# A lead of 16 slots in place of 12 between dots and scaling, and the gelu of a batch at step 2 in place of step 4

## The chip, the core and the metric

The kernel runs on one core of one Trainium2 chip. The core has five engines with a program each: TensorE (PE: PE's matmuls and PEld's weight loads), VectorE (DVE), ScalarE (ACT), GpSimd (POOL) and SyncE (SP), and 16 DMA engines that move data between memory and the on-chip buffers. The engines wait for each other by semaphores. The metric is the device time of one execution in microseconds (us).

## What is computed

One encoder layer over 1024 tokens of width 1024, all in float32: a LayerNorm, a mixer (attention over latents with 8 heads, and a Fourier branch, merged by gates), a LayerNorm, and the channel part, in which each token takes 128 single-neuron experts out of 16,384:

```python
def peer(x, w_q, keys, w_u, w_v):
    xt = x.reshape(T, D)
    q = (xt @ w_q).reshape(T, PEER_HEADS, 2, PEER_HALF)
    s_half = jnp.einsum('thcd,hcnd->thcn', q, keys, ...)
    sv, si = lax.top_k(s_half, PEER_TOPK)
    cand = (sv[:, :, 0, :, None] + sv[:, :, 1, None, :]).reshape(...)
    cv, ci = lax.top_k(cand, PEER_TOPK)
    ...
    expert = (ia * PEER_NKEYS + ib).reshape(T, PEER_HEADS * PEER_TOPK)
    gate = jax.nn.softmax(cv, axis=-1).reshape(T, PEER_HEADS * PEER_TOPK)
    def run(blk):
        xc, ec, gc = blk
        u = jnp.take(w_u, ec, axis=0)
        h = jnp.einsum('cd,ced->ce', xc, u, ...)
        a = (jax.nn.gelu(h, approximate=False) * gc).astype(x.dtype)
        return jnp.einsum('ce,ced->cd', a, jnp.take(w_v, ec, axis=0))
```

For each token and each of its 128 experts a row of w_u (4 KB) and a row of w_v (4 KB) are read: 1024 x 128 x 2 x 4 KB, or 1.07 GB, of the 1.24 GB that the core moves in all.

## The kernel before

The 1024 tokens are four groups of two tiles of 128 tokens. A tile has 128 slots, one for each of a token's experts: slot i of a tile is the i-th expert of all of its 128 tokens, one on each partition. One gather (an indirect DMA that GpSimd starts) brings one row of w_u, or of w_v, to each partition, 512 KB. A group has 256 slots.

A slot passes five stations: GpSimd gathers its u row (L310); DVE multiplies it with the token and sums it up, the dot (L872); GpSimd gathers its v row (L319); ACT scales it by the slot's coefficient into one of two buffers av (L1099); PE adds it to acc by eight transposing matmuls (L600). Between dot and scaling, for eight slots at a time (a batch), ACT takes the gelu of the eight dots (L1090) and DVE multiplies it with the gates to the coefficients (L883). The scaling of a batch's first slot waits for them.

The order is written out by hand. Each engine runs through steps m = 0 to 255 of a group. At step m GpSimd gathers the u row of slot m + LEAD + AHEAD and then the v row of slot m + LEAD; DVE does the dot of slot m + LEAD + AHEAD; ACT scales, and PE adds, slot m + LEAD. LEAD is 64. A slot number past 255 is one of the next group, so the numbers run on from group to group. At step m of a batch's eight (m modulo 8) ACT takes the gelu at 4, DVE the coefficients at 5, both for the batch that starts at the next step 0. In one engine's program the steps follow in order; between engines there are only the semaphores.

There are six buffers for u rows and six for v rows. GpSimd waits at slot i for the dot of slot i - 6 (u_free) or for the scaling of slot i - 6 (scaled).

Beside this work of group g each engine does the "front" of group g + 1 in the same steps: attention in steps 0 to about 72 (scores, maximum on DVE at L760, exponential on ACT at L1030 every four steps, transposes, values), gates in 72 to 120 (sigmoid L1047), output projection to 136, LayerNorm, then queries of the experts to about 215. The group before all this (steps 0 to 255 of the first front) has no retrieval beside it till its own expert numbers are there. After the last group's start there is no front.

The expert numbers of a tile come from DVE in four pairs of heads, 32 slots each (`retrieve`): two top-16 searches for each head, and for each pair the numbers at L852, which gives the semaphore `handed`, the token's copy (L855) and the softmax of the gates, with an exponential on ACT at L1083. Tile 0 has its pairs at steps 171, 187, 203 and 219 of the front; tile 1 at steps 45, 69, 93 and 117 of the next round. The first gather of each 32 slots waits for `handed`. HAND0 and HAND1, worked out from AHEAD, are the steps at which the first gathers of tile 0 and tile 1 stand; ACT's load of the residual rows stands at step HAND1 + 2.

Of the kernel before, what the change touches and what calls it, by code (L numbers as in the profile page):

```python
# [35 lines left out]
SLOTS = PH * TOPK  # L36
STEPS = TILES * SLOTS
BATCH = 8
AHEAD = 12
LEAD = 64  # L40
PAIRS = PH // 2
PSLOTS = SLOTS // PAIRS
# [17 lines left out]
IDS = 3  # L60
HAND1 = SLOTS - AHEAD - LEAD
HAND0 = STEPS - AHEAD - LEAD
assert T0 + T_PERIOD + IDS + 3 < HAND0 and T_PERIOD <= PSLOTS // 2 and T0 + PH * T_PERIOD <= STEPS
# [4 lines left out]
def layer_program(nc, x, lnp, w_lat, w_z, w_kr, b_lat, b_zT, b_krT, gqkv, w_uk, w_uv, b_gate, wstream,  # L68
# [4 lines left out]
    with ctx:  # L73
# [168 lines left out]
        def has_slot(g, i, last):  # L242

            return i < STEPS and not (isinstance(g, int) and g < 0) or i >= STEPS and not last
# [45 lines left out]
        def _(pool):  # L290
# [13 lines left out]
            def gather_u(g, i):  # L304
                g, i = slot_of(g, i)
                if i % PSLOTS == 0:
                    pool.wait_ge(handed, g * TILES * PAIRS + i // PSLOTS + 1)
                pool.wait_ge(u_free, g * STEPS + i + 1)
                t, s = divmod(i, SLOTS)
                pool.indirect_dma_start(  # L310
                    u_rows[:, ring(g, i, NU), :], None, peer_u,
                    bass.IndirectOffsetOnAxis(ap=ids_peer[:, t, s:s + 1], axis=0)).then_inc(u_in[ring(g, i, NU)], 16)
# [10 lines left out]
            def peer(g, last):  # L323
                for m in range(STEPS):
                    if has_slot(g, m + LEAD + AHEAD, last):
                        gather_u(g, m + LEAD + AHEAD)
                    if has_slot(g, m + LEAD, last):
# [303 lines left out]
        def _(dve):  # L631
# [234 lines left out]
            def dot(g, i):  # L866
                g, i = slot_of(g, i)
                t = i // SLOTS
                dve.wait_ge(u_in[ring(g, i, NU)], landed(g, i, NU))
                row = u_rows[:, ring(g, i, NU), :]  # L870
                b = i // BATCH % 2
                v.tensor_tensor_reduce(out=row, in0=row, in1=h1_peer[:, t, :], scale=1.0, scalar=0.0, op0=ALU.mult,  # L872
                                       op1=ALU.add, accum_out=dots[:, b, i % BATCH:i % BATCH + 1]).then_inc(u_free, 1)
# [23 lines left out]
            def peer(g, m, last):  # L897
                if has_slot(g, m + LEAD + AHEAD, last):
                    dot(g, m + LEAD + AHEAD)
                if m % BATCH == 5 and has_slot(g, m + LEAD + BATCH, last):  # L900
                    coefs(g, (m + LEAD) // BATCH + 1)
# [42 lines left out]
        def _(act):  # L944
# [42 lines left out]
            for n in range(2 * FG):  # L987
                g, half = divmod(n, 2)
# [5 lines left out]
            for n in range(1, TT * FG, 2):  # L994
                tt, g = divmod(n, FG)
# [3 lines left out]
            for n in range(H):  # L999
                pair, half = divmod(n, 2)  # L1000
                act.wait_ge(k_ps, n + 1)
                for odd in range(2):
                    last = s.activation(KT[0:NOPE, 2 * pair + odd, half * 512:(half + 1) * 512],
                                        (m0, m1)[n % 2][odd * NOPE:(odd + 1) * NOPE, :], ACT.Copy)
# [81 lines left out]
            def gelu(g, k):  # L1086
                g, i = slot_of(g, k * BATCH)
                k = i // BATCH
                act.wait_ge(u_free, g * STEPS + NU + BATCH * (k + 1))
                s.activation(act_out[:, k % 2, :], dots[:, k % 2, :], ACT.Gelu).then_inc(act_done, 1)  # L1090
# [38 lines left out]
                        act.wait_ge(y_spilled[i], 16 * (FG // 2))  # L1129

            def gelus(g, m, last):
                if m % BATCH == 4 and has_slot(g, m + LEAD + BATCH, last):
                    gelu(g, (m + LEAD) // BATCH + 1)

            for m in range(STEPS):
                if has_slot(-1, m + LEAD, False):
                    scale(-1, m + LEAD)
                gelus(-1, m, False)
                front(0, m)
                dft(m)  # L1140

            def group(g, last):
                for m in range(STEPS):
                    for t in range(TILES):
                        if m + LEAD == (t + 1) * SLOTS:
                            evict(g, t)
                    if has_slot(g, m + LEAD, last):
                        scale(g, m + LEAD)
                    gelus(g, m, last)
                    gate_exp(g, 1, m, R0, R_PERIOD)  # L1150
                    if not last:
                        front(g + 1, m)
                    for t in range(TILES):
                        if m + LEAD == (t + 1) * SLOTS:
                            finish(g, t)
                        if m + LEAD == (t + 1) * SLOTS + 2:
                            store(g, t)
# [89 lines left out]
```

## Time and profile before

| | us |
|---|---|
| median of three runs | 3777.69 |
| lowest and highest | 3771.69 to 3777.8 |
| profiled execution, its own time | 3777.35 |
| its span in the trace | 3775.5 |
| busy: PE 2722.5, POOL 2360.9, DVE 2217.4, ACT 1600.3 | 72%, 63%, 59%, 42% of the span |
| q0, the gathers' DMA queue | 75.2% of 16 engines' span |
| first gather starts | 530.8 |
| mean granted TensorE clock | 0.808 of full speed |

The first 530 us are projections of all tokens and the first front; from there to the end the gathers run. A row of the profile names the line, the engine, the operation and `out<-in` by the program's names (`rows` holds the u and v buffers, `dots`, `coef`, `av` as above; `small` holds the row maximum among others). Behind a group, or in square brackets behind a row, stands the idle time of the engine before it, and what ended it. "issue" is a wait for nothing that the profile shows, "remote" one for something that it doesn't name. Times are from the start of the span.

### The profile page before, as it was taken

The numbers are of one execution on the slowest core, as the hardware profiler recorded it, in microseconds if no ns is written. First come the engines' busy times: TensorE is split into PE (matmuls) and PEld (weight loads), VectorE is DVE, ScalarE is ACT, GpSimd is POOL, SyncE is SP. The second block draws the span as 40 slices with busy tenths as digits, with TensorE's granted clock in tenths as the row PEclk, the third lists the DMA queues.
The fourth block names the chain that finished last, engine by engine and source line by source line (L and its number), as shares of the span: only waits on it lengthen the run. The fifth ranks groups of instructions, "written<-read, shape, count | busy, mean of one in ns | idle before, by whom it ended". The sixth has DMA issues, their size and how long they took to land.

```text
span 3775.5 us, 40818 instructions
## 1 busy us (share of the span) xinstructions
PE 2722.5 (72%) x14008; PEld 2179.7 (58%) x14008; DVE 2217.4 (59%) x5004; ACT 1600.3 (42%) x1836; POOL 2360.9 (63%) x2075
## 2 busy tenths in 40 slices
PE   6999966578788676577887775677986665565545
PEld 3456745456675565466775664566765554444444
DVE  5143067458765676477765685578655774467533
ACT  1121014345454444354554454454544453344434
POOL 4000028766677767766677787756776777677775
PEclk9999987578799886698898895787998885655656
DMA  4235459998999999998999999989999999999997
GB/s 167 86 106 173 151 171 353 356 348 314 345 409 409 392 363 356 362 342 330 358 409 404 375 379 350 359 319 331 399 409 391 381 343 351 349 357 345 353 359 291
DMA packets 350432, 1240.83 MB, mean 329 GB/s; under 512 B 38480, under 2 KB 46160, under 8 KB 349712
## 3 DMA queue, kind: packets, MB, share of 16 engines
q0 software_dynamic: 294912, 1073.87, 75.2%
q1 hardware_dynamic: 34096, 117.94, 8.5%
q10 hardware_dynamic: 21216, 46.40, 3.4%
q8 instruction: 111, 1.82, 0.2%
q14 instruction: 97, 0.79, 0.1%
HBM read 1222.33 MB, written 15.73 MB: 328 GB/s over the span
## 4 chain that ended last, share of the span: by engine, by line
PE 29%; POOL 24%; issue 13%; another core or an unknown queue 10%; DMA 8%; ACT 7%; DVE 6%; DVEq 3%; SPq 0%; ACTq 0%
POOL rows L319 12%; POOL rows L310 11%; PE acc L600 9%; DMA rows<-in_peer_v,ids_peer 7%; ACT av L1099 5%; PE fA L523 3%; PE m L567 2%; PE fA L483 2%; PE m L371 2%; PE m L499 2%; PE acc L589 1%; DVE rows L872 1%; PE fB L341 1%; PE fB L535 1%
## 5 line engine op out<-in xcount | busy, mean ns | idle before, releaser
L600 PE MATMUL acc<-ident,av 128*128 128x128 f32 x8192 | 1394.9, 331 | 904.3 <-ACT av L1099 587.2
L600 PEld LDWEIGHTS acc<-ident,av 128*128 128x128 f32 x8192 | 1176.8, 172 | 1137.8 <-ACT av L1099 692.5
L1099 ACT ACTIVATE av<-rows,coef 128x1024 f32<-128x1024 f32 x1024 | 1161.4, 1145 | 1479.6 <-DMA rows<-in_peer_v,ids_peer 563.5
L310 POOL DMA_INDIRECT rows<-in_peer_u,ids_peer x1024 | 1137.2, 1111 | 807.3 <-DVE ids_peer L852 339.5
L872 DVE CUSTOM_DVE_ANT_0 rows<-rows,hh 128x1024 f32<-128x1024 f32 x1024 | 1235.7, 1222 | 651.3 <-DMA rows<-in_peer_u,ids_peer 573.8
L319 POOL DMA_INDIRECT rows<-in_peer_v,ids_peer x1024 | 1175.6, 1148 | 444.0 <-issue 292.4
L567 PE MATMUL m<-hT_g,wring 128*128 128x256 f32 x1024 | 249.2, 400 | 1.1 <-ACT hT_g L1061 1.1
L523 PE MATMUL fA<-hT_g,wring 128*128 128x256 f32 x1024 | 241.7, 392 | 0.9 <-issue 0.9
L567 PEld LDWEIGHTS m<-hT_g,wring 128*128 128x128 f32 x1024 | 203.4, 204 | 29.7 <-ACT hT_g L1061 1.5
L523 PEld LDWEIGHTS fA<-hT_g,wring 128*128 128x128 f32 x1024 | 199.1, 199 | 29.0 <-issue 2.4
L768 DVE COPY S<-fB 128x1024 f32<-128x1024 f32 x64 | 78.2, 1222 | 151.9 <-PE fB L341 69.1
L499 PEld LDWEIGHTS m<-V,S 128*128 128x128 f32 x1024 | 145.1, 225 | 13.6 <-DVE S L768 7.8
L499 PE MATMUL m<-V,S 128*128 128x64 f32 x1024 | 146.2, 306 | 7.1 <-DVE S L768 6.6
L483 PE MATMUL fA<-KT,hT_g 96*128 96x512 f32 x256 | 131.5, 636 | 4.2 <-issue 4.0
L1030 ACT ACTIVATE S<-fA,small 128x1024 f32<-128x1024 f32 x64 | 71.0, 1110 | 117.0 <-DVE small L762 116.2
L535 PE MATMUL fB<-yo,wring 128*128 128x256 f32 x512 | 115.8, 379 | 0.0
L883 DVE TENSOR_TENSOR coef<-act_out,gate_peer 128x8 f32<-128x8 f32 x128 | 21.1, 165 | 140.1 <-ACT act_out L1090 86.0
L535 PEld LDWEIGHTS fB<-yo,wring 128*128 128x128 f32 x512 | 95.4, 190 | 12.0
L783 DVE TENSOR_TENSOR prod<-sg,fB 128x512 f32<-128x512 f32 x32 | 21.9, 683 | 135.9 <-PE fB L535 94.4
L760 DVE TENSOR_REDUCE small<-fA 128x1 f32<-128x1024 f32 x64 | 78.1, 1221 | 35.3 <-PE fA L483 17.4
L1090 ACT ACT_TABLE_LOAD x73 | 93.7, 1283 | 1.3
L341 PE MATMUL fB<-ident,S 128*128 128x128 f32 x512 | 83.4, 315 | 3.7 <-issue 3.6
(153 smaller groups left out, 2173.5 us busy)
## 6 DMA issues: line engine op xcount, KB each, us to landing
wring<-in_wstream SPq DMA_DIRECT2D x192, 512.0 KB
ln<-in_dft_seq ACTq DMA_DIRECT2D x32, 512.0 KB, 3.4
rows<-in_peer_u,ids_peer POOLq DMA_INDIRECT x1024
rows<-in_peer_v,ids_peer POOLq DMA_INDIRECT x1024
hT_g<-in_x SPq DMA_DIRECT2D x8, 512.0 KB, 3.6
hres_spill<-KT ACTq DMA_DIRECT2D x8, 512.0 KB, 2.7
hT_spill<-rows ACTq DMA_DIRECT2D x1, 4096.0 KB
wring<-in_wstream SPq DMA_DIRECT2D x16, 256.0 KB
```

Of the source, the lines that this page charges most:

```text
L310: pool.indirect_dma_start(u_rows[:, ring(g, i, NU), :], None, peer_u, bass.IndirectOffsetOnAxis(ap=ids_peer[:, t, s:s + 1], axis=0)).then_ ...
L319: pool.indirect_dma_start(v_rows[:, ring(g, i, NV), :], None, peer_v, bass.IndirectOffsetOnAxis(ap=ids_peer[:, t, s:s + 1], axis=0)).then_ ...
L341: return nc.tensor.transpose(out_, in_, ident[:, :])
L483: last = mm(fA[:, half * 512:(half + 1) * 512], qT_g[0:QK, h, tok(qt)], KT[0:QK, h, half * 512:(half + 1) * 512], start=True, stop=True)
L499: last = mm(m1[:, h * VD:(h + 1) * VD], probsT[:, tok(k)], V[:, k, h * VD:(h + 1) * VD], start=k == 0, stop=k == TT - 1)
L523: last = mm(gb[:, j * GROUP:(j + 1) * GROUP], w[:, tok(k)], hT_g[:, k, :], start=k == 0, stop=k == KD - 1)
L535: last = mm(yb[:, j * GROUP:(j + 1) * GROUP], w[:, tok(4 * j + k)], src[:, k, :], start=k == 0, stop=k == 3)
L567: last = mm(m0[:, (qc % 2) * GROUP:(qc % 2 + 1) * GROUP], w[:, tok(k)], hT_g[:, k, :], start=k == 0, stop=k == KD - 1)
L600: last = mm(acc[:, tok(k)], av[:, i % NAV, tok(k)], ident[:, :], is_transpose=True, start=i % SLOTS == 0 and k % 4 == 0, stop=i % SLOTS == ...
L872: v.tensor_tensor_reduce(out=row, in0=row, in1=h1_peer[:, t, :], scale=1.0, scalar=0.0, op0=ALU.mult, op1=ALU.add, accum_out=dots[:, b, i ...
L1090: s.activation(act_out[:, k % 2, :], dots[:, k % 2, :], ACT.Gelu).then_inc(act_done, 1)
L1099: s.activation(av[:, i % NAV, :], v_rows[:, ring(g, i, NV), :], ACT.Copy, scale=coef[:, b, i % BATCH:i % BATCH + 1]).then_inc(scaled, 1)
```

## The change

AHEAD goes from 12 to 16, and the gelu of a batch goes from step 4 of eight to step 2.

```diff
@@ -36,7 +36,7 @@
 BATCH = 8
-AHEAD = 12
+AHEAD = 16
 LEAD = 64
@@ -1129,7 +1129,7 @@
             def gelus(g, m, last):
-                if m % BATCH == 4 and has_slot(g, m + LEAD + BATCH, last):
+                if m % BATCH == 2 and has_slot(g, m + LEAD + BATCH, last):
                     gelu(g, (m + LEAD) // BATCH + 1)
```

The dot of slot i now stands four steps earlier among all other instructions of DVE, and its u gather four earlier on GpSimd. The last dot that a gelu needs stood one step before it and now stands three before; the coefficients stood one step behind it and now stand three behind. HAND1 goes from 52 to 48 and HAND0 from 180 to 176; the load of the residual rows goes from step 54 to 50. The numbers of instructions stay as they are, but for ACT's table loads, which the compiler puts in wherever the next function is in another table: 164 before, 162 now.

On GpSimd (POOL) the first gathers of all stand like this before (L310 gathers u rows, L319 v rows):

```order
L310 DMA rows<-in_peer_u,ids_peer 128x1024 [waits u_free,handed]
L310 DMA rows<-in_peer_u,ids_peer 128x1024 [waits u_free] x12
L319 DMA rows<-in_peer_v,ids_peer 128x1024 [waits scaled]
L310 DMA rows<-in_peer_u,ids_peer 128x1024 [waits u_free]
L319 DMA rows<-in_peer_v,ids_peer 128x1024 [waits scaled]
```

and now:

```order
L310 DMA rows<-in_peer_u,ids_peer 128x1024 [waits u_free,handed]
L310 DMA rows<-in_peer_u,ids_peer 128x1024 [waits u_free] x16
L319 DMA rows<-in_peer_v,ids_peer 128x1024 [waits scaled]
L310 DMA rows<-in_peer_u,ids_peer 128x1024 [waits u_free]
L319 DMA rows<-in_peer_v,ids_peer 128x1024 [waits scaled]
```

Seventeen u gathers stand ahead of the first v gather, where there were thirteen, and at the other end of the program sixteen v gathers stand alone where there were twelve.

On DVE, round steps 44 to 47 beside the attention of the next group, before. The numbers of tile 1's first pair are written at L852; `u_landed` with a number is the buffer whose row the dot waits for:

```order
L872 ISA rows,dots<-rows,hh 128x1024 [waits u_landed1]
L872 ISA dots 128x1
L883 TENSOR_TENSOR coef<-act_out,gate_peer 128x8 [waits scaled,act_done]
L852 SCALAR_TENSOR_TENSOR ids_peer<-cab 128x32
L855 COPY hh<-hh 128x1024
L857 TENSOR_REDUCE small<-gate_front 128x2 [waits gexp_done]
L859 RECIPROCAL small<-small 128x2
L861 TENSOR_TENSOR gate_peer<-gate_front,small 128x32
L872 ISA rows,dots<-rows,hh 128x1024 [waits u_landed2]
L872 ISA dots 128x1
L872 ISA rows,dots<-rows,hh 128x1024 [waits u_landed3]
```

and now:

```order
L872 ISA rows,dots<-rows,hh 128x1024 [waits u_landed5]
L872 ISA dots 128x1
L883 TENSOR_TENSOR coef<-act_out,gate_peer 128x8 [waits scaled,act_done]
L852 SCALAR_TENSOR_TENSOR ids_peer<-cab 128x32
L855 COPY hh<-hh 128x1024
L857 TENSOR_REDUCE small<-gate_front 128x2 [waits gexp_done]
L859 RECIPROCAL small<-small 128x2
L861 TENSOR_TENSOR gate_peer<-gate_front,small 128x32
L872 ISA rows,dots<-rows,hh 128x1024 [waits u_landed0]
L872 ISA dots 128x1
L872 ISA rows,dots<-rows,hh 128x1024 [waits u_landed1]
```

They read alike, with dots of other slots: the one ahead of L852 was that of slot 121 and is now that of slot 125, so the numbers, which slot 128 is the first to need, come two slots ahead of that gather where they came six.

On ACT, in a piece of the same attention (L1099 scaling, L1025 a copy of queries, L1030 the exponential, L1090 the gelu), before:

```order
L1099 ACTIVATE av<-rows,coef 128x1024 x3
L1030 ACTIVATE S,rowsum<-fA,small 128x1024
L1099 ACTIVATE av<-rows,coef 128x1024
L1025 ACTIVATE hT_g<-m 64x256
L1099 ACTIVATE av<-rows,coef 128x1024 x3
L1090 ACT_TABLE_LOAD
L1090 ACTIVATE act_out<-dots 128x8
L1030 ACT_TABLE_LOAD
L1030 ACTIVATE S,rowsum<-fA,small 128x1024
L1099 ACTIVATE av<-rows,coef 128x1024
```

and now:

```order
L1099 ACTIVATE av<-rows,coef 128x1024 x3
L1030 ACTIVATE S,rowsum<-fA,small 128x1024
L1099 ACTIVATE av<-rows,coef 128x1024
L1025 ACTIVATE hT_g<-m 64x256
L1099 ACTIVATE av<-rows,coef 128x1024
L1090 ACT_TABLE_LOAD
L1090 ACTIVATE act_out<-dots 128x8
L1099 ACTIVATE av<-rows,coef 128x1024 x2
L1030 ACT_TABLE_LOAD
L1030 ACTIVATE S,rowsum<-fA,small 128x1024
```

The gelu and its table load stand two scalings earlier; the load for the exponential stays in front of the exponential.

## Rows read from the trace of the kernel before

**Rows 1.** The page, the span in 40 equal slices: DMA tenths and GB/s.

```profile
DMA  4235459998999999998999999989999999999997
GB/s 167 86 106 173 151 171 353 356 348 314 345 409 409 392 363 356 362 342 330 358 409 404 375 379 350 359 319 331 399 409 391 381 343 351 349 357 345 353 359 291
```

**Rows 2.** Windows: us, busy of PE, PEld, DVE, ACT, POOL, PE clock, DMA share, GB/s.

```profile
650.00:755.00 105.00, 56.73 (x280) 46.67 (x279) 45.37 (x83) 41.65 (x41) 78.72 (x71) 0.60 0.94 349
775.00:1025.00 250.00, 196.25 (x1125) 168.43 (x1124) 182.93 (x392) 133.20 (x152) 159.51 (x146) 0.81 0.90 328
1025.00:1250.00 225.00, 182.40 (x987) 147.84 (x985) 137.73 (x301) 110.36 (x115) 164.33 (x145) 0.93 1.03 409
```

**Rows 3.** Waits of the whole kernel: who waited for whom, us, times, longest.

```profile
ACT av L1099 <- remote: 427.0, 99, 12.1
POOL rows L310 <- DVE dots L872: 166.5, 72, 5.9
DVE coef L883 <- ACT act_out L1090: 86.0, 24, 10.6
DVE coef L883 <- issue: 53.8, 17, 8.4
...
ACT act_out L1090 <- DVE dots L872: 7.4, 2, 7.2
```

**Rows 4.** Timeline of the first dots and the first v gather: start, duration.

```profile
539.09 1.20 DVE L872 CUSTOM_DVE_ANT_0 rows<-rows,hh 128x1024 f32<-128x1024 f32 x1
540.22 1.22 DVE L872 CUSTOM_DVE_ANT_0 rows<-rows,hh 128x1024 f32<-128x1024 f32 x1
...
559.21 0.94 POOL L319 DMA_INDIRECT rows<-in_peer_v,ids_peer  x1 [0.30 <-issue]
```

**Rows 5.** Timeline of GpSimd over the last gathers.

```profile
3725.07 1.25 POOL L310 DMA_INDIRECT rows<-in_peer_u,ids_peer  x1 [0.30 <-issue]
...
3735.45 1.02 POOL L319 DMA_INDIRECT rows<-in_peer_v,ids_peer  x1 [0.31 <-issue]
...
3754.47 0.93 POOL L319 DMA_INDIRECT rows<-in_peer_v,ids_peer  x1 [0.30 <-issue]
```

**Rows 6.** Timeline: gathers of step 48 and numbers of step 45, first and last time.

```profile
910.54 0.94 POOL L310 DMA_INDIRECT rows<-in_peer_u,ids_peer  x1 [1.34 <-DVE dots L872]
...
921.96 0.19 DVE L852 SCALAR_TENSOR_TENSOR ids_peer<-cab 128x32 int32<-128x32 f32 x1
...
931.81 1.21 DVE L872 CUSTOM_DVE_ANT_0 rows<-rows,hh 128x1024 f32<-128x1024 f32 x1
...
3342.09 0.19 DVE L852 SCALAR_TENSOR_TENSOR ids_peer<-cab 128x32 int32<-128x32 f32 x1
...
3343.31 0.94 POOL L310 DMA_INDIRECT rows<-in_peer_u,ids_peer  x1 [0.30 <-issue]
```

**Rows 7.** Timeline: the u gather with the shortest way to its dot.

```profile
3616.92 1.99 POOL L310 DMA_INDIRECT rows<-in_peer_u,ids_peer  x1 [0.30 <-issue]
...
3621.99 1.23 DVE L872 CUSTOM_DVE_ANT_0 rows<-rows,hh 128x1024 f32<-128x1024 f32 x1 [1.59 <-DMA rows<-in_peer_u,ids_peer]
```

**Rows 8.** Timeline round a v row that came late.

```profile
3613.22 1.15 ACT L1099 ACTIVATE av<-rows,coef 128x1024 f32<-128x1024 f32 x1 [10.08 <-remote]
...
3614.50 0.17 DVE L883 TENSOR_TENSOR coef<-act_out,gate_peer 128x8 f32<-128x8 f32 x1 [10.59 <-ACT act_out L1090]
...
3614.64 1.97 POOL L319 DMA_INDIRECT rows<-in_peer_v,ids_peer  x1 [4.96 <-ACT av L1099]
```

**Rows 9.** Timeline of ACT round a gelu beside attention.

```profile
857.54 1.15 ACT L1099 ACTIVATE av<-rows,coef 128x1024 f32<-128x1024 f32 x1 [3.52 <-PE acc L600]
...
858.71 1.28 ACT L1090 ACT_TABLE_LOAD   x1
...
860.01 0.21 ACT L1090 ACTIVATE act_out<-dots 128x8 f32<-128x8 f32 x1
...
861.53 1.11 ACT L1030 ACTIVATE S<-fA,small 128x1024 f32<-128x1024 f32 x1
```

## The prediction

> **What bounds the kernel now.** I read the page's slices first. From the sixth slice on the DMA digits are nearly all 9, while PE, DVE, ACT and POOL stand between 3 and 8 [rows 1]: the rows of the expert tables are what the kernel waits for, and all else has room on average. Then the stretches [rows 2]. There are three kinds. With the next group's gates and output projection beside the retrieval (1025 to 1250 us) the DMA engines are full and move 409 GB/s. With gathers almost alone (650 to 755 us) they are busy 94% of the time at 349 GB/s. With the attention of the next group beside it (775 to 1025 us) the share falls to 0.90 and DVE is the busiest engine but PE, at 182.9 of 250 us; the same stretch comes back twice (from about 1590 and 2400 us). Only there does the order of the work cost transfers, some 25 us of idle DMA in each, 75 us in all. That is the pot from which a better order could draw, or to which a worse one would add.
>
> Third, the waits [rows 3]. The change acts on the tie between DVE and ACT: ACT's gelu waits for eight dots, DVE's coefficients wait for the gelu. The first wait is 7.4 us in the whole kernel. The second is 86.0 us in 24 waits and 53.8 us more put down to issue: 139.8 us. GpSimd, which starts every transfer, waits for dots 166.5 us. ACT waits 427.0 us, up to 12.1 us at a time, on something the profile doesn't name; [rows 8] shows what such a wait is.
>
> **What the lead really changes.** The 16 is a count of slots, not of buffers. The u rows have six buffers before and after, so at step m GpSimd still may be at most six steps ahead of DVE, and at most six ahead of ACT through the v rows. No more rows are in flight. What moves is (a) how many dots stand alone at the start and how many scalings stand alone at the end, (b) four steps' less room between the writing of expert numbers on DVE and the first gather that needs them, (c) the gelu, now three steps behind its last dot and three ahead of its coefficients, before one and one.
>
> **(a) Start.** The second head's top-16 ends where the first dot starts, at 539.09 us, and dots follow each other in 1.13 us (540.22 less 539.09) [rows 4]. Steps 176 to 179 have no retrieval work on DVE, so four more dots stand there back to back: the rest of DVE's program, and the first v gather (559.21 us, which waits behind the u gathers in GpSimd's order), comes 4 x 1.13 = 4.5 us later. Their rows are already in the six buffers. Cost +4.5 us; at least 0, if the four gathers brought forward are simply saved later in a DMA-bound stretch.
> **End.** Steps 176 to 179 of the last group lose their u gather. The last four steps with both took 3735.45 - 3725.07 = 10.4 us; steps with a v gather alone run at 0.93 + 0.30 = 1.23 us, or (3754.47 - 3735.45) / 11 = 1.73 us as they really went with a late row among them [rows 5]. Four of them: 4.9 to 6.9 us. Gain 3.5 to 5.5 us, I take 4.4. Start and end together: +0.1.
>
> **(b) The expert numbers.** In tile 1 the first pair is written at DVE's step 45. Its first gather was at GpSimd's step 52 and is now at 48. With six steps of room, 52 could never be early; 48 can. The trace shows it: the gather of step 48 (then slot 124) started at 910.54 us, the numbers were written at 921.96 + 0.19 = 922.15 us [rows 6]. So GpSimd will stand 11.6 us where before it went on, and with it the v gather queued behind. This pattern stands in three groups, the three with attention beside it; in the last group the numbers (3342.09 us) were there before the gather of step 48 (3343.31 us). In tile 0 the margin is 5 steps (171 to 176), and outside the attention stretches GpSimd isn't that far ahead of DVE, so I cost it at nothing; with the cover gone it is one step, some 3 us.
> What does an 11.6 us stop cost? Rows already fetched feed DVE for steps 46 and 47. The shortest time from a u gather's start to its dot is 5.07 us (3616.92 to 3621.99) [rows 7]. Step 51's row, three steps of 2 x (0.94 + 0.30) = 2.48 us behind 922.15, lands at about 922.15 + 7.4 + 5.1 = 934.7 us, against its dot at 931.81 us [rows 6]: DVE is 2.9 us late there. ACT was three steps ahead of DVE and loses that lead. DVE is idle a quarter of this stretch, so part is made up. I take half, 1.5 us a group, +4.5 us in all. The ends are 0 and 3 x 11.6 = 34.8 us.
>
> **(c) The gelu.** Take a late v row [rows 8]: ACT got its row after 10.08 us, ran the gelu behind it, and DVE's coefficients had waited 10.59 us. With the gelu at step 2 DVE would have gone on. But GpSimd's next v gather waited for that same scaling (4.96 us), not for DVE, and its next u gather needs a dot that was already done. After the stall DVE works off its rows in 1.13 us each while GpSimd needs 2.48 us a step. So most of the 139.8 us is wait that nobody pays for. In the three attention stretches, where DVE's time does count, I can lay only a few us of it. Gain 3 us; between 0 and 35, a quarter of it.
> On ACT the program has 162 table loads for 164; in attention, gelu and exponential come to stand apart: before, load, gelu, load, exponential ran in one piece from 858.71 to 861.53 us [rows 9], now load and gelu come two steps earlier, so every second exponential can start 1.5 us sooner. It then feeds transposes which PE reaches after other work (its next group starts behind a scaling that also comes later), so nothing counted; at the most 24 x 1.5 = 36 us. Two loads fewer, 2 x 1.28 = 2.6 us on an engine that is half idle: nothing.
> In [rows 9] the load starts 0.02 us after the scaling's end and the gelu 0.02 us after the load. The Trainium skill ("ScalarE: Activation LUTs", What ACT_TABLE_LOAD costs) adds a drain of about 1.38 us to each 1.283 us load. By it two loads fewer would be worth 5.3 us of ACT; the rows show the load's length to the hundredth and no such drain before or behind it, so 2.6 us stands, hidden either way.
>
> **Sum.** 0.1 + 4.5 - 3 = +1.6 us on the profiled execution's own 3777.35 us (span 3775.5 and 1.85 around it), which lies 0.3 us from the median 3777.69: 3779 us.
>
> **Rivals.**
> *The softer tie pays.* If the DVE wait behind late rows does delay GpSimd, the gain is up to a quarter of 139.8 us, 35, with some of the exponential's room. For it: GpSimd does wait 166.5 us for dots. Against: those waits lie in the attention stretches, the coefficient waits mostly outside. Middle value -20 with (b): about 3758 us.
> *The expert numbers hold GpSimd.* If the DMA time lost in the 11.6 us isn't made up before the full stretch at 1025 us (where nothing can be made up, the engines being at 409 GB/s), each group loses 5 to 11.6 us. It decides from 2.5 us a group. Middle value 8 x 3 = +24: about 3801 us. For it: the stop comes where DVE is busiest. Against: the stretch behind it still has 10% idle DMA.
> *The gathers alone set the time.* If the order hardly matters since the DMA engines are full, the change is +-3 us, 3777 us; this shares the forecast's case.
> In [rows 2] two full rates stand side by side, 409 and 349 GB/s. The Trainium skill ("DMA: Bandwidth & Descriptors", Where 436 GB/s comes from) says that for transfers from HBM the HBM side binds at about 358 GB/s per core and the ports at 435. By 358 the gather stretches at 349 would be within 3% of the end, and no order of instructions could win anything there. 409 GB/s in this trace is above it, so it isn't the bound here, and the first rival keeps its chance.
>
> **How the numbers follow.** What measurement can tell from no change is about 0.2%, 7.5 us. Forecast (with the third rival) 0.45: 3772 to 3787. Softer tie 0.29. Expert numbers 0.26. Faster takes the first rival and a little of the forecast's lower edge, less its own small gains: 0.30. Slower: 0.27. Same: 0.43. The range for 8 in 10 takes in both rivals' middle values and a bit over: 3750 to 3803.
>
> **What would show it.** Right: between about 910 and 925 us GpSimd has one wait of some 10 us before the gather of slot 128, released by the expert numbers (line 852), and so in the next two groups; the coefficients' wait (line 883) falls by over a half while GpSimd's waits for scalings stay near 150 us; the first v gather comes 4 to 5 us later, and the last 16 gathers are v alone. Wrong: the DMA share of 775 to 1025 us moves by over 0.02 either way; GpSimd's wait for dots falls by tens of us (first rival) or the time to the end of each attention stretch grows by over 5 us (second).

## The result, and the profile after

Six runs of each on the same chip, in turns: 3800.3 us for the changed kernel against 3777.7 us, ratio 1.0067, with a 95% interval of [1.0039, 1.0095]. The change makes the kernel slower, by 23 us going by the medians and 25 us by the ratio. The forecast was 3779 us; the time lies near that of the rival "the expert numbers hold GpSimd" (3801 us). The profiled execution took 3794.7 us, span 3792.9.

The page of the changed kernel, DMA tenths and GB/s in 40 slices of 94.8 us, answers to [rows 1]:

```profile
DMA  4235459987999999999999999979999999998997
GB/s 170 83 106 176 148 175 354 364 334 280 345 410 409 403 376 356 344 336 330 392 409 405 384 376 368 338 282 329 396 408 391 377 349 350 354 362 314 351 369 285
```

Read the tenth slice (853 to 948 us) and the twenty-seventh (2466 to 2560 us): 280 GB/s where 314 stood, and 282 where 319 stood. They are the end of the first and of the third attention stretch. The nineteenth slice, at the same place in the second group, has 330 in both. Single slices differ as much elsewhere (392 for 358 in the twentieth, 314 for 345 in the thirty-seventh), so the slices only point at the place. Now its windows (columns as in [rows 2]):

```profile
650.00:755.00 105.00, 62.64 (x295) 51.25 (x293) 52.26 (x98) 44.37 (x44) 79.98 (x73) 0.60 0.96 363
775.00:1025.00 250.00, 181.35 (x1068) 150.27 (x1069) 175.23 (x367) 128.80 (x146) 151.20 (x140) 0.83 0.86 314
1025.00:1250.00 225.00, 194.82 (x1031) 158.44 (x1029) 141.89 (x322) 111.94 (x120) 163.43 (x146) 0.92 1.02 402
```

The DMA share of the attention stretch fell from 0.90 to 0.86, which is over the 0.02 that the prediction named as a sign of being wrong, and DVE did 367 instructions for 392. The clock didn't do it: 0.83 granted here, 0.81 before. The full stretch behind it gives nothing back. The place of the loss shows in 30 us of it. Two windows of before, then the same two of the changed kernel:

```profile
910.00:940.00 30.00, 23.14 (x144) 19.91 (x144) 28.25 (x64) 18.64 (x21) 19.71 (x19) 0.83 0.88 308
940.00:1025.00 85.00, 65.83 (x351) 58.96 (x352) 63.13 (x145) 43.73 (x49) 56.54 (x49) 0.76 0.92 335
```

```profile
910.00:940.00 30.00, 22.17 (x123) 18.75 (x122) 25.58 (x60) 14.87 (x18) 11.35 (x11) 0.78 0.43 141
940.00:1025.00 85.00, 60.32 (x346) 52.46 (x345) 61.78 (x138) 42.17 (x48) 55.99 (x51) 0.78 0.94 351
```

From 910 to 940 us GpSimd did 11 instructions for 19, and the DMA engines moved 141 GB/s for 308, so 5.0 MB less. In the 85 us behind it 1.4 MB came back. The waits of the whole kernel (who for whom, us, times, longest), which answer to [rows 3]:

```profile
DVE rows L872 <- DMA rows<-in_peer_u,ids_peer: 643.6, 384, 5.0
ACT av L1099 <- remote: 500.8, 124, 10.5
POOL rows L310 <- DVE ids_peer L852: 376.8, 4, 341.4
...
POOL rows L319 <- ACT av L1099: 169.9, 112, 5.3
POOL rows L310 <- DVE dots L872: 137.3, 59, 6.3
...
DVE coef L883 <- ACT act_out L1090: 16.7, 4, 9.5
...
DVE coef L883 <- issue: 6.8, 5, 3.3
```

Two things happened as foreseen. The coefficients' wait for the gelu fell from 139.8 us to 16.7 + 6.8 = 23.5. And GpSimd now waits for expert numbers four times: once at the very start (341.4 us, there before too), and three times more, 376.8 - 341.4 = 35.4 us in all. Its waits for dots fell from 166.5 to 137.3 us. The prediction had named such a fall as a sign of the first rival, but here it comes with a longer time: where GpSimd stands for the numbers it no longer stands for a dot. Two more profiles of before have 175.5 and 192.5 us of these waits. The first of the three in the timeline (start, duration, wait before it and releaser), where [rows 6] show before:

```profile
930.24 0.19 DVE L852 SCALAR_TENSOR_TENSOR ids_peer<-cab 128x32 int32<-128x32 f32 x1
930.70 1.15 POOL L310 DMA_INDIRECT rows<-in_peer_u,ids_peer  x1 [14.28 <-DVE ids_peer L852]
931.75 1.22 DVE L872 CUSTOM_DVE_ANT_0 rows<-rows,hh 128x1024 f32<-128x1024 f32 x1
932.15 1.63 POOL L319 DMA_INDIRECT rows<-in_peer_v,ids_peer  x1 [0.30 <-issue]
...
937.87 1.15 ACT L1099 ACTIVATE av<-rows,coef 128x1024 f32<-128x1024 f32 x1 [6.93 <-DMA rows<-in_peer_v,ids_peer]
939.07 1.27 PE L600 MATMUL acc<-ident,av 128*128 128x128 f32 x8 [3.34 <-ACT av L1099]
940.08 1.22 DVE L872 CUSTOM_DVE_ANT_0 rows<-rows,hh 128x1024 f32<-128x1024 f32 x1 [2.24 <-issue]
...
942.83 1.23 DVE L872 CUSTOM_DVE_ANT_0 rows<-rows,hh 128x1024 f32<-128x1024 f32 x1 [1.52 <-DMA rows<-in_peer_u,ids_peer]
...
945.33 1.23 DVE L872 CUSTOM_DVE_ANT_0 rows<-rows,hh 128x1024 f32<-128x1024 f32 x1 [1.27 <-DMA rows<-in_peer_u,ids_peer]
```

GpSimd stood 14.28 us for numbers that DVE wrote at its step 45. The v gather of the same step stood behind it, so ACT waited 6.93 us for its next v row, PE's accumulation 3.34 us late behind ACT, and DVE then waited three steps in a row for u rows, though in the profile of before it has no such wait from 917 to 957 us. The chain of waits of the same execution goes straight through it (start, duration, what):

```profile
930.24 0.20 DVE ids_peer L852
930.44 0.26 issue
930.70 1.15 POOL rows L310
931.84 0.30 issue
932.15 5.65 DMA rows<-in_peer_v,ids_peer
...
937.87 1.16 ACT av L1099
```

It passes through the v row, not the u row; DVE's late u rows lie beside it. The two later stops of this execution are 6.84 and 14.28 us long. In tile 0 and in the last group there is none.

### The profile page after: what moved, and what is told of

Same layout as the page of the kernel before. It is cut to its first block, busy times and chain, and to the rows that moved or that the text cites. A ratio compares the mean times of both kernels' runs of the same rounds, so it can differ in the third digit from the quotient of the medians.

```text
span 3792.9 us, 40816 instructions
## 1 busy us (share of the span) xinstructions
PE 2730.0 (72%) x14008; PEld 2180.2 (57%) x14008; DVE 2218.2 (58%) x5004; ACT 1597.4 (42%) x1834; POOL 2355.5 (62%) x2075
## 4 chain that ended last, share of the span: by engine, by line
PE 32%; POOL 23%; issue 13%; another core or an unknown queue 10%; ACT 8%; DMA 7%; DVE 4%; DVEq 2%; SPq 0%; ACTq 0%; POOLq 0%
POOL rows L319 12%; POOL rows L310 11%; PE acc L600 11%; DMA rows<-in_peer_v,ids_peer 6%; ACT av L1099 6%; PE fA L523 3%; PE m L567 3%; PE fA L483 2%; PE m L499 2%; PE fB L535 2%; PE m L371 2%; PE acc L589 1%; PE fB L341 1%; DVE rows L872 1%
## 5 line engine op out<-in xcount | busy, mean ns | idle before, releaser
L1099 ACT ACTIVATE av<-rows,coef 128x1024 f32<-128x1024 f32 x1024 | 1161.6, 1145 | 1492.6 <-DMA rows<-in_peer_v,ids_peer 547.5
L310 POOL DMA_INDIRECT rows<-in_peer_u,ids_peer x1024 | 1138.1, 1111 | 811.5 <-DVE ids_peer L852 376.8
L319 POOL DMA_INDIRECT rows<-in_peer_v,ids_peer x1024 | 1169.2, 1142 | 461.8 <-issue 291.9
L567 PE MATMUL m<-hT_g,wring 128*128 128x256 f32 x1024 | 257.3, 409 | 1.1 <-ACT hT_g L1061 1.1
L535 PE MATMUL fB<-yo,wring 128*128 128x256 f32 x512 | 125.4, 398 | 7.9 <-issue 7.6
L1030 ACT ACTIVATE S<-fA,small 128x1024 f32<-128x1024 f32 x64 | 71.0, 1110 | 113.1 <-DVE small L762 111.9
L341 PEld LDWEIGHTS fB<-ident,S 128*128 128x128 f32 x512 | 69.2, 158 | 28.2 <-issue 28.2
```

The lines of the kernel that those rows point to most:

```text
L310: pool.indirect_dma_start(u_rows[:, ring(g, i, NU), :], None, peer_u, bass.IndirectOffsetOnAxis(ap=ids_peer[:, t, s:s + 1], axis=0)).then_ ...
L319: pool.indirect_dma_start(v_rows[:, ring(g, i, NV), :], None, peer_v, bass.IndirectOffsetOnAxis(ap=ids_peer[:, t, s:s + 1], axis=0)).then_ ...
L341: return nc.tensor.transpose(out_, in_, ident[:, :])
L535: last = mm(yb[:, j * GROUP:(j + 1) * GROUP], w[:, tok(4 * j + k)], src[:, k, :], start=k == 0, stop=k == 3)
L567: last = mm(m0[:, (qc % 2) * GROUP:(qc % 2 + 1) * GROUP], w[:, tok(k)], hT_g[:, k, :], start=k == 0, stop=k == KD - 1)
L1099: s.activation(av[:, i % NAV, :], v_rows[:, ring(g, i, NV), :], ACT.Copy, scale=coef[:, b, i % BATCH:i % BATCH + 1]).then_inc(scaled, 1)
```

## The experiments

All ratios are to the kernel before, run in turns with the others on the same chip. The chips are of two kinds (last section), so a ratio is never formed across chips. "Stop" is GpSimd's wait for the expert numbers of tile 1. The runs fall into four questions.

**Is it the stop, the lead itself, or the gelu?** Four kernels:

```
earlier numbers: the change, and   R0, R_PERIOD = 23, 12    (27 before)
lead alone:      AHEAD = 16, gelu at m % BATCH == 4
gelu alone:      AHEAD = 12, gelu at m % BATCH == 2
later numbers:   kernel before, and R0, R_PERIOD = 31, 12
```

Expected of earlier numbers: 

> Lead 16 and gelu at step 2 as in the changed kernel, with R0 from 27 to 23: tile 1's expert numbers are written four steps earlier, at step 41, seven steps ahead of their first gather as in the kernel before. Theory A (the cost is GpSimd's stop for the numbers): GpSimd's waits for L852 beside the first one (35.4 us in the changed kernel's profile) go to 0, and the time goes back to 3775 to 3785 us, ratio to before 0.999 to 1.002. Theory B (the cost is the lead: four more dots at the start, the gelu far from its dots): waits gone, but the time stays at 3793 us or more, ratio 1.004 to 1.008. Theory C (the gelu's place on ACT): the same as B.

Expected of the lead alone: 

> The lead of 16 alone, gelu left at step 4. Theory A: as slow as the full change, 3793 to 3805 us, with 25 to 40 us of waits for L852. Theory B: the same time. Theory C: back to 3775 to 3785 us.

Expected of the gelu alone: 

> The gelu at step 2 alone, lead left at 12, so that ACT's gelu needs a dot that DVE does one step later. Theory A and B: no wait for L852; the time moves only by what ACT's wait for the dots costs (7.4 us in all before, now some tens of us spread over 128 gelus, ACT being 42% busy), 3775 to 3790 us. Theory C: 3793 us or more with ACT's waits for dots still under 10 us.

Expected of later numbers: 

> The kernel before with R0 from 27 to 31 and nothing else: tile 1's numbers at step 49, three steps ahead of the first gather at step 52, as in the changed kernel. Theory A: waits for L852 of 20 to 40 us beside the first, time 3790 to 3802 us, ratio 1.004 to 1.007. Theory B and C: 3772 to 3783 us, ratio within 0.2% of 1.

Measured, before at 3561.6 us:

| kernel | us | ratio | GpSimd's waits for numbers, tile 1 |
|---|---|---|---|
| earlier numbers | 3557.4 | 0.9988 [0.9965, 1.0010] | none (tile 0: 3 x 3.28) |
| lead alone | 3586.7 | 1.0078 [1.0050, 1.0107] | 10.51, 9.38, 9.73 |
| gelu alone | 3559.1 | 0.9986 [0.9964, 1.0008] | none |
| later numbers | 3568.2 | 1.0011 [0.9989, 1.0034] | 6.76, 6.76, 8.00 |

The lead alone makes the whole loss; with the numbers four steps earlier the same lead and the same gelu lose nothing that can be measured. So it is neither the start, nor the end, nor the gelu. In tile 0, where the prediction saw one step of margin left "with the cover gone", both kernels with a lead of 16 have three short waits here, of at most 3.28 us. The first stop of the lead alone:

```profile
893.69 1.14 POOL L310 DMA_INDIRECT rows<-in_peer_u,ids_peer  x1 [10.51 <-DVE ids_peer L852]
```

The gelu alone shows a wait that nobody pays for. Its waits of the whole kernel:

```profile
ACT act_out L1090 <- DVE dots L872: 219.6, 105, 8.6
...
POOL rows L310 <- DVE dots L872: 78.3, 54, 3.3
POOL rows L319 <- ACT av L1099: 39.6, 109, 1.1
```

With the gelu at step 2 and a lead of 12 ACT waits 219.6 us for the last of eight dots, where it waited 7.4 us in [rows 3], and the kernel isn't slower.

"Later numbers" was a miss. It has the same margin of 3 steps as the change (numbers at step 49, first gather at 52) and its stops sum to 21.5 us, as expected, but its time can't be told from before. The stops are shorter, 7 us for 10 to 14. Moving R0 shifts retrieval work as well, here and in "earlier numbers", so neither is a clean test of the stop.

**Does the stop do it without the lead?** The change again, and the kernel before with nothing but the wait put in, on a chip of the first kind (before at 3819.0 us):

```
 in gather_u:
+                if i == SLOTS - 4:
+                    pool.wait_ge(handed, g * TILES * PAIRS + PAIRS + 1)
```

Expected of the change again: 

> The changed kernel itself, on the chip of this call. Theory A (GpSimd's stop for tile 1's numbers, at lead 16): 25 to 35 us of waits for L852 beside the first, the three attention stretches (scaling of slot 64 to that of slot 128 of a group's round) together 25 to 30 us longer than with the numbers early, ratio 1.005 to 1.009, as with the lead alone (1.0078). Rival theory D (the gelu's new place makes up part of it): ratio 1.001 to 1.004.

Expected of the stop alone: 

> The kernel before with one wait more on GpSimd: it waits for tile 1's numbers (handed, written at step 45) already before the u gather of its step 48, slot 124 of tile 0, where the changed kernel has to. Order, lead and buffers are those of before. Theory A: waits for L852 of 20 to 35 us beside the first and ratio 1.004 to 1.008. Rival theory E (the stop hurts only together with the lead of 16, since moving the numbers to step 49 at lead 12 gave 1.0011 with 21.5 us of waits): ratio 0.999 to 1.003.

The change again came to 3844.5 us, 1.0080 [1.0051, 1.0109], with stops of 14.28, 13.94 and 14.28 us; the stop alone to 3850.5 us, 1.0101 [1.0068, 1.0135], with 13.22, 13.93 and 14.29 us. Both sums, 42.5 and 41.4 us, lie above what was expected. On another chip (before at 3823.3 us) the stop alone was run again:

Expected: 

> The stop alone at lead 12, as run before on another chip (1.0101). Both kinds of rows are late behind it. Theory A: 1.006 to 1.012 on this chip too.

It took 3854.9 us, 1.0085 [1.0051, 1.0118], with four stops, 13.20, 13.94, 14.27 and 10.50 us. At a lead of 12, with dots, scalings and gelu where they always were, one added wait gives the whole loss, on two chips. The first group of its first run:

```profile
926.80 0.19 DVE L854 SCALAR_TENSOR_TENSOR ids_peer<-cab 128x32 int32<-128x32 f32 x1
...
927.26 1.14 POOL L312 DMA_INDIRECT rows<-in_peer_u,ids_peer  x1 [13.22 <-DVE ids_peer L854]
...
934.54 1.15 ACT L1101 ACTIVATE av<-rows,coef 128x1024 f32<-128x1024 f32 x1 [7.04 <-DMA rows<-in_peer_v,ids_peer]
...
935.74 1.97 PE L602 MATMUL acc<-ident,av 128*128 128x128 f32 x8 [4.83 <-ACT av L1101]
936.29 1.23 DVE L874 CUSTOM_DVE_ANT_0 rows<-rows,hh 128x1024 f32<-128x1024 f32 x1 [1.89 <-DMA rows<-in_peer_u,ids_peer]
```

Line for line it is the picture of the changed kernel (lines lie two further down): 13.22 for 14.28, ACT 7.04 for 6.93, PE 4.83 for 3.34.

How large the loss is can also be estimated from the slices, against a profile of before on the same chip. Expected: 

> The kernel before, one look, so that there is a trace of it from the same chip as the others of this call. No wait for L852 beside the first; the three attention stretches together within 5 us of 547 us if the chip is like that of the last call, some 646 us if it is like that of the first.

It has no wait for the numbers but the first. Counted from the scaling of step 0 to that of step 64, the three attention stretches take 662 us together, against 697 in the change again; the chip is like the first.

GB/s of that profile of before (slices of 95.1 us), then of the change again (96.5 us):

```profile
GB/s 166 86 100 171 151 171 357 363 330 323 333 404 408 380 385 362 336 335 317 362 409 407 379 354 341 348 327 319 393 408 386 381 339 365 348 349 356 351 337 306
```

```profile
GB/s 171 78 109 175 152 190 343 357 331 292 316 402 405 372 381 349 329 338 290 341 405 408 372 368 357 349 324 283 375 409 399 377 338 353 349 358 326 341 354 299
```

The tenth, nineteenth and twenty-eighth slices hold the three stops: 323 to 292, 317 to 290, 319 to 283. As a share of a slice that is (323-292)/323 x 96.5 = 9.3 us, and 8.2 and 10.9 us: 28.4 us, against 3844.5 - 3819.0 = 25.5 us by the medians and 30.6 by the ratio. That they agree so well is in part luck: these two executions are 53 us apart (3860.4 and 3807.2 us), and the three slices of another profile of before have 311, 331 and 326.

**What of the stop costs: late u rows, late v rows, or both?** Here I had priced only u rows. The first kernel is the change with the v gathers of four steps put ahead of the stop:

```
+                    if m == HAND1 and has_slot(g, m + LEAD, last):
+                        for n in range(m, m + 4):
+                            gather_v(g, n + LEAD)
 ...
-                    if has_slot(g, m + LEAD, last):
+                    if has_slot(g, m + LEAD, last) and not HAND1 <= m < HAND1 + 4:
```

Expected: 

> The changed kernel, with the v gathers of steps 48 to 51 put ahead of the u gather of step 48 on GpSimd, so that they go out before the stop. If the stop costs through the v gathers queued behind it (ACT's scaling of step 48 waited 6.9 us for its row in the changed kernel's profile): most of the loss goes, ratio 0.999 to 1.003, with the waits for L852 as long as before. If it costs through the u rows and DVE: ratio stays at 1.005 to 1.009.

It took 3812.0 us, 0.9993 [0.9970, 1.0016], on the chip on which the change took 1.0080. The loss is gone with the lead at 16 and the gather of slot 128 still after the numbers. Its timeline there:

```profile
930.75 1.04 POOL L319 DMA_INDIRECT rows<-in_peer_v,ids_peer  x1 [6.60 <-ACT av L1102]
...
933.05 0.19 DVE L855 SCALAR_TENSOR_TENSOR ids_peer<-cab 128x32 int32<-128x32 f32 x1
933.51 1.14 POOL L310 DMA_INDIRECT rows<-in_peer_u,ids_peer  x1 [1.72 <-DVE ids_peer L855]
...
940.82 1.23 DVE L875 CUSTOM_DVE_ANT_0 rows<-rows,hh 128x1024 f32<-128x1024 f32 x1 [0.15 <-DMA rows<-in_peer_u,ids_peer]
```

GpSimd still stands, 6.60 us for a v buffer and 1.72 us for the numbers; that its wait for the numbers would stay as long was a miss. But by then four v gathers are out that in the change followed the stop, and behind it those of u go out back to back without a v gather between; so DVE waits 0.15 us here, and the order has cured the late u rows along with the late v rows.

Then both halves apart, at lead 12. "V late" sends the u gathers of steps 48 to 51 first, waits, and sends the v gathers (a second edit, left out here, skips those u gathers in their old place); "u late" is the stop alone with the v gathers of those steps ahead of it.

```
v late:
+                    if m == HAND1 - 4 and has_slot(g, m + LEAD, last):
+                        for n in range(m, m + 4):
+                            gather_u(g, n + LEAD + AHEAD)
+                        pool.wait_ge(handed, g * TILES * PAIRS + PAIRS + 1)
```

Expected of v late: 

> The same stop, but the u gathers of steps 48 to 51 go out ahead of it, so that only the v gathers stand behind it. If the v rows carry the cost: nearly that of the stop with both, 1.005 to 1.010. If the u rows do: under 1.003.

Expected of u late: 

> The same stop with the v gathers of steps 48 to 51 ahead of it, so that only u gathers stand behind it (1.0032 in the last call). If the v rows carry the cost: 1.000 to 1.004, less than half of the stop with both. If the u rows do: as much as with both.

V late took 3831.3 us, 1.0020 [0.9997, 1.0043]; u late 3824.6 us, 0.9998 [0.9968, 1.0028]; on the same chip the stop on both was 1.0085. Each half costs less than the stop on both. By what was expected, v late speaks for the u rows and u late for the v rows as the cause, so neither alone is it. V late in the first group:

```profile
926.54 0.19 DVE L856 SCALAR_TENSOR_TENSOR ids_peer<-cab 128x32 int32<-128x32 f32 x1
926.64 0.93 POOL L310 DMA_INDIRECT rows<-in_peer_u,ids_peer  x1 [2.20 <-DVE dots L876]
927.88 0.93 POOL L319 DMA_INDIRECT rows<-in_peer_v,ids_peer  x1 [0.30 <-issue]
...
933.30 1.15 ACT L1103 ACTIVATE av<-rows,coef 128x1024 f32<-128x1024 f32 x1 [6.06 <-DMA rows<-in_peer_v,ids_peer]
```

The v gathers go out as late as in the stop alone (928.71 us there) and ACT waits 6.06 us for its row, 7.04 there, but the kernel hardly pays. So ACT's late row by itself isn't the price. In this kernel no wait of GpSimd's but the first is put down to the numbers; it waits for dots instead. What neither half does is to make DVE late as in the stop alone, as the table below shows.

U late had been run once before, on another chip (before at 3558.0 us). Expected: 

> The same early wait as in the stop alone (kernel before, lead 12, GpSimd waits for tile 1's numbers before the u gather of step 48), but with the v gathers of steps 48 to 51 ahead of it. If the stop costs only through the v gathers behind it: ratio 0.998 to 1.003, against 1.0101 of the stop alone, and the three attention stretches (scaling of slot 64 to 120) within 10 us of the kernel before on the same chip. If the u rows carry part of the cost: 1.004 or more.

There it gave 3567.9 us, 1.0032 [1.0010, 1.0054]. This interval doesn't hold 1 and that of the second run does, so what is left of the stop in it stays open, between nothing and 0.5%. With the one run the two halves add up to 0.18%, with the other to 0.52%, against 0.85%: whether the stop on both costs more than this sum isn't shown.

A profile of before on the chip of the halves was taken, to have its gathers beside theirs. Expected: 

> The kernel before, one look for its trace on this chip: no wait for L852 but the first.

It has no such wait. The timelines of all these profiles give three counts. "Empty" is GpSimd's idle time beyond the usual 0.31 us between two gathers, from 25 us before the writing of tile 1's first numbers to 12 us behind it. "DVE late" is its waits for u rows in the 20 us behind the writing. Both are means of three groups. "Steps 40 to 64" is the time from the scaling of step 40 to that of step 64, the three groups together. All but the ratio are from one execution each.

| kernel | empty, us | DVE late, us | steps 40 to 64, us | ratio |
|---|---|---|---|---|
| first kind of chip: before, three profiles | 12.6, 12.9, 11.5 | 0 | 246, 252, 248 | 1 |
| the change, first result | 15.4 | 4.9 | 262 | 1.0067 |
| the change again | 19.3 | 4.9 | 284 | 1.0080 |
| stop alone, twice | 18.5, 20.3 | 4.6, 4.8 | 280, 288 | 1.0101, 1.0085 |
| v late | 14.9 | 0 | 270 | 1.0020 |
| u late | 14.3 | 1.0 | 261 | 0.9998 |
| v gathers first | 14.1 | 0.8 | 256 | 0.9993 |
| second kind: gelu alone | 0 | 0.2 | 213 | 0.9986 |
| earlier numbers | 3.5 | 0 | 215 | 0.9988 |
| lead alone | 9.6 | 5.0 | 237 | 1.0078 |
| later numbers | 6.9 | 4.7 | 231 | 1.0011 |
| u late, first run | 4.0 | 1.0 | 223 | 1.0032 |

The loss lies where the stop is: steps 40 to 64 take 31 to 39 us more in the change again and in the stop alone than the 249 us of before, the mean of three. V late has 21 more and u late 12, which together is as much as the stop on both. Of the two candidates, GpSimd's empty time and DVE's late rows, the ratios alone choose neither, since both are high in the dear kernels and low in the cheap ones. Two cases speak for the empty time. In the first result's second group, with the stop of 6.84 us, DVE was 5.04 us late and ACT 6.91, as in the first group, but GpSimd was empty for only 6.5 us, and steps 40 to 64 took 81.8 us for 82.5 before. In v late DVE was never late, and its profile still has 270 us (at 3850.7 us of its own, though, 19 above that kernel's median). No kernel moved one of the two and held the other, so this is argued, not shown.

**How much lead is free, and is there a better version?** Three more, before at 3558.0 us:

```
lead 14:               AHEAD = 14, gelu at m % BATCH == 2
v before u:            kernel before, gather_v ahead of gather_u in every step
gelu, numbers earlier: AHEAD = 12, gelu at 2, R0 = 23
```

Expected of lead 14: 

> Lead 14, gelu at step 2: numbers at step 45, first gather at step 50, five steps of room (seven before, three in the change). By the stop theory the wait is the one of the change (14 us) less two steps of about 3.4 us each: 5 to 8 us a group, with two steps more of v rows gathered ahead, so ACT hardly starves: ratio 1.000 to 1.004. If the lead itself cost (two of the four dots at the start and more), 1.003 to 1.005 with no row of ACT late behind the stop.

Expected of v before u: 

> The kernel before with the two gathers of every step in the other order on GpSimd: v row first, then u row. If ACT's v rows are the tighter of the two everywhere in the attention stretches (their lateness is what made the stop dear), this gives 5 to 20 us: ratio 0.995 to 0.999. If the DMA engines' rate sets the pace and the order within a step doesn't matter: 0.998 to 1.002. If DVE's rows get late by it: above 1.002.

Expected of gelu and earlier numbers: 

> Lead 12, gelu at step 2 and tile 1's numbers at step 41: each of the two alone or with lead 16 gave ratios of 0.9986 and 0.9988, neither clear of 1. If they are small gains that add up: 0.995 to 0.998. If neither is one: 0.998 to 1.002.

In that order they took 3556.0 us, 0.9994 [0.9975, 1.0014]; 3555.3 us, 0.9984 [0.9965, 1.0003]; 3552.9 us, 0.9988 [0.9968, 1.0008]. With 5 steps of margin the stops of tile 1 are 3.35, 4.71 and 2.06 us, shorter than the 5 to 8 expected, and cost nothing that can be measured. V before u lies in both ranges that were named for it and doesn't decide between them, and the gelu and the earlier numbers are no gains that add up. No kernel beats the one before for certain: all three intervals, and those of the gelu alone and of earlier numbers, hold 1.

## Why the prediction was wrong

**Right: the stop and its place.** The margin of 3 steps, the gather of slot 128, three groups and not the last, tile 0 free: all came out. The length was worked out as 11.6 us; the three stops are 14.28, 6.84 and 14.28, mean 11.8. That the mean fits is luck: in the change again it is 14.2. The working began at the gather's start, 910.54 us, behind a wait of 1.34 us, and took the numbers' time of before, 922.15; in the changed kernel GpSimd was idle from 916.42 us and the numbers were there at 930.43.

**Wrong: the price of (b).** It was put at 1.5 us a group, 4.5 us in all, between ends of 0 and 34.8. The change costs 23 to 31 us by the medians and ratios of its two results, the stop alone 32 to 39. That is 8 to 13 us a group, 60 to 95% of the stops' length; the upper end, not the lower, was the nearer. The step that failed is the one in which the stop's price was taken from the u row of step 51 alone ("DVE is 2.9 us late there ... I take half"). DVE was late three times in a row, by 2.24, 1.52 and 1.27 us, 5.0 us in all, over three times the 1.5 charged. And the same stop holds the v stream. "ACT ... loses that lead" stood in the text, and was counted as nothing; ACT was then 6.93 us late and PE behind it. The runs show that one wait ahead of both streams gives the whole loss (1.0101 and 1.0085), and that with either stream let past it the cost is between nothing and 0.5%. The reading that fits them best is that GpSimd's time is what is gone: behind the stop both streams are refilled at one pair in 2.48 us, and from 940 to 1025 us only 1.4 of the 5.0 MB came back. DVE's three late steps, up to 15 us in the three groups, remain as a rival to it. The prediction's second rival had the price nearly right, and its condition too: what isn't made up before the full stretch at 1025 us is lost. It was given 8 us a group and 0.26. The argument held against it, 10% idle DMA behind the stop, didn't hold: the full stretch has none (1.03), and in the rest of the attention stretch, 940 to 1025 us, the share only went from 0.92 to 0.94.

**Start and end (a).** The first v gather came 566.75 - 532.30 = 34.45 us behind the first u gather:

```profile
532.30 1.35 POOL L310 DMA_INDIRECT rows<-in_peer_u,ids_peer  x1 [341.39 <-DVE ids_peer L852]
...
566.75 0.94 POOL L319 DMA_INDIRECT rows<-in_peer_v,ids_peer  x1 [0.30 <-issue]
...
572.20 1.15 ACT L1099 ACTIVATE av<-rows,coef 128x1024 f32<-128x1024 f32 x1 [10.23 <-DVE coef L883]
```

Before it was 559.21 - 530.82 = 28.39. That is 6.1 us later for 4.5 predicted: the dots that stand together there don't all run back to back, as the fifth and sixth wait 0.30 and 1.01 us for their u rows. The last 16 gathers are v alone as forecast. Start, end and gelu together are what earlier numbers show: 0.9988, so at most a few us of either sign.

**The gelu (c).** -3 us predicted; alone it measures 0.9986 [0.9964, 1.0008], -5 us with 0 inside. In the changed kernel 116 us of coefficient waits went and nothing that can be measured was got for them. The rival "the softer tie pays" (3758 us) is out: its -20 us would be 0.9947, and earlier numbers, with the same lead and gelu and no stop in tile 1, has 0.9988 [0.9965, 1.0010].

**The order (third rival).** That order hardly matters isn't true in attention: one wait moved 0.85 to 1%. For the gather stretches no run contradicts it; v before u, which swaps the gathers of every step, has 0.9984 [0.9965, 1.0003].

**Left open.** Why the stops of 7 us in later numbers cost so little. The table has steps 40 to 64 there at 231 us, 16 to 18 more than in the gelu alone and in earlier numbers, so the stops aren't free where they stand; in its profile steps 64 to 120 then took 532 us for 546 and 542 in those two. But v before u has 534 there with R0 unmoved, so that the shifted retrieval gives it back isn't shown. The second stop of the changed kernel was 6.84 us in one profile and 13.94 in the other. In the first GpSimd had issued for 30 us up to the stop without waiting for a buffer, so it was less far ahead; what had held it back wasn't tried.

## What to carry to other kernels

A wait put before one instruction of an engine that runs its program in order stops all streams that the engine feeds. Price it by the issue time that it empties, over all streams, and not by the first consumer that comes late: here that gave 1.5 us a group for 8 to 13. Where several streams share the issuing engine, what doesn't need the late data can go ahead of the wait: reordering four gathers bought back the whole 0.8%. Widening a lead eats the margin to every producer that has a fixed place in the order of steps; here a lead of 14 with 5 steps of margin lost nothing that can be measured, and a lead of 16 with 3 lost 0.7 to 0.8%.

## What the runs showed of the hardware

Before took 3778 to 3823 us on some chips and 3558 to 3562 us on others, 6 to 7% less, the same program. The profiles show two differences. ACT's waits for v rows put down to "remote" are 427 to 622 us on the first and none on the others, and the granted TensorE clock is 0.79 to 0.81 on the first and 0.82 to 0.84 on the others. The change again, on a chip of the first kind:

```profile
ACT av L1099 <- remote: 621.5, 135, 13.3
```

V before u, on one of the second, has in its waits only

```profile
ACT av L1099 <- DMA rows<-in_peer_v,ids_peer: 1064.9, 661, 4.4
```

with none over 4.4 us. All in all ACT doesn't wait less for v rows there (1065 us, against 427.0 and 563.5 us in the profile of before); what differs is the length of single waits, up to 12 to 13 us on the first kind. Why they are so long on some chips, and whether they or the clock make the 6 to 7%, no run tells. The changed kernel itself ran on the first kind only (1.0067 and 1.0080); the lead alone, on the second, lost as much (1.0078).
